# Key/value projection and compressed pages of a decoder step on TensorE: products in fp32 replaced by three products of rounded parts

## What is computed

```
def key_side(h):
    kv = (rms_norm(h, kv_norm) @ w_kv).reshape(B, T, 3, 2, N_KV, HEAD_DIM)      # 1024 -> 3 branches x 512
    return kv[:, :, 0], kv[:, :, 1], kv[:, :, 2]
def seg_proj(seg):                                                            # runs of 16 tokens
    first = jnp.einsum('bsjcgd,cjde->bscge', seg, cmp_w[:, :CMP_STRIDE])
    second = jnp.einsum('bsjcgd,cjde->bscge', seg, cmp_w[:, CMP_STRIDE:])
    return first, second
def compress_blocks(first, second, L):
    blk = first[:, :nc] + second[:, 1:nc + 1] + cbias[:, None, :]
    kc = rms_norm(blk[:, :, 0], k_norm[0])
    return kc, blk[:, :, 1], e_pos
...
past_c = cache_cmp_kv[page_table]         # 8 samples x 32 pages of 128 tokens, 256 KB a page
```

## Time and profile before

| | us |
|---|---|
| median of 3 runs (2642.25 to 2648.58) | 2647.62 |
| the profiled execution, its own time | 2653.37 |
| its span, first to last instruction | 2651.6 |
| TensorE busy | 2437.2 (92%) |
| VectorE busy | 1385.0 (52%) |
| ScalarE busy | 904.4 (34%) |
| GpSimd busy | 774.1 (29%) |

### The profile page before, as it was taken

How to read it: one execution, slowest core, us unless ns; L and a number is a source line. 1 busy time by engine, 2 the same in 40 slices (tenths; PEclk the granted TensorE clock), 3 DMA queues, 4 the chain that set the end, 5 groups by cost and what they waited for, 6 DMA issues and landing times. The chain is left out here.

```text
span 2651.6 us, 62243 instructions
## 1 busy us (share of the span) xinstructions
PE 2437.2 (92%) x25616; PEld 1985.1 (75%) x25616; DVE 1385.0 (52%) x2833; ACT 904.4 (34%) x2023; POOL 774.1 (29%) x460
## 2 busy tenths in 40 slices
PE   5999799986899999989999898997999978999998
PEld 3777699965799999944544385565766677999998
DVE  7216665536577773022233435774777746777600
ACT  2205344315222121110101145765888822222210
POOL 0001000110267665200000023772222204677641
PEclk8999899967899999999999987997999988999999
DMA  2121000012122223151898310005777612222231
GB/s 106 55 64 57 8 4 12 28 39 90 59 72 79 87 74 119 49 221 47 323 326 280 118 58 1 2 1 185 253 251 251 224 64 67 79 87 79 94 99 61
DMA packets 109448, 276.58 MB, mean 104 GB/s; under 512 B 13657, under 2 KB 14554, under 8 KB 107290
## 3 DMA queue, kind: packets, MB, share of 16 engines
q1 hardware_dynamic: 109210, 273.19, 30.5%
HBM read 264.42 MB, written 16.97 MB: 106 GB/s over the span
## 5 line engine op out<-in xcount | busy, mean ns | idle before, releaser
L319 PE MATMUL ps<-parts 128*128 128x288 f32 x6144 | 815.1, 295 | 7.4 <-POOL parts L288 7.4
L319 PEld LDWEIGHTS ps<-parts 128*128 128x128 f32 x6144 | 814.2, 188 | 8.1 <-POOL parts L288 8.1
L288 POOL TENSOR_TENSOR parts<-kept,parts 128x1024 fp32r<-128x1024 f32 (+1 forms) x120 | 320.7, 2673 | 119.5 <-ACT parts L283 112.3
L293 POOL TENSOR_TENSOR parts<-kept 128x1024 fp32r<-128x1024 f32 (+1 forms) x92 | 191.5, 2081 | 378.2 <-DMA kept<-in_wall 188.6
L1660 PE MATMUL ps<-mix,kept 128*128 128x512 f32 (+1 forms) x544 | 228.4, 579 | 0.3 <-DMA mix<-in_cmp_pool 0.3
L1660 PEld LDWEIGHTS ps<-mix,kept 128*128 128x128 f32 x544 | 101.4, 194 | 120.8 <-issue 119.7
L2292 POOL TENSOR_SCALAR mix<-mix 128x128 f32<-128x128 f32 (+3 forms) x128 | 136.7, 1087 | 71.9 <-DVE mix L2266 71.8
L288 POOL TENSOR_TENSOR query_rounded<-mix,query_rounded 128x1024 fp32r<-128x1024 f32 x8 | 16.0, 2000 | 466.8 <-ACT query_rounded L283 466.8
L2769 POOL TENSOR_TENSOR mix<-mix 128x512 f32<-128x512 f32 x64 | 67.0, 1047 | 252.7 <-ACT mix L2793 197.9
L1599 DVE TENSOR_TENSOR kept<-kept,ps 128x576 f32<-128x576 f32 x16 | 12.1, 756 | 245.9 <-PE ps L319 245.9
L702 PE MATMUL ps<-mix 128*128 128x288 f32 x512 | 126.4, 410 | 2.7 <-DVE mix L507 2.4
(11 more groups left out here) (470 smaller groups left out, 4870.0 us busy)
## 6 DMA issues: line engine op xcount, KB each, us to landing
mix<-in_cmp_pool SPq DMA_DIRECT2D x256, 256.0 KB, 4.9
mix<-in_slc_pool SPq DMA_DIRECT2D x192, 256.0 KB, 3.7
kept<-in_wall SPq DMA_DIRECT2D x88, 512.0 KB, 3.5
mix<-in_wall SPq DMA_DIRECT2D x48, 512.0 KB, 3.5
kept<-in_wdown SPq DMA_DIRECT2D x32, 704.0 KB, 4.1
kept<-in_slc_pool SPq DMA_DIRECT2D x64, 256.0 KB, 3.8
out_s_win<-in_state_win SPq DMA_DIRECT2D x1, 8064.0 KB
mix<-in_wkv SPq DMA_DIRECT2D x8, 768.0 KB, 10.3
```

The lines of the kernel that those rows point to most:

```text
L288: return e.tensor_tensor(low.bitcast(F32R), whole, high, ALU.subtract)
L293: e.tensor_tensor(high.bitcast(F32R), whole, c.c("one").to_broadcast([P, whole.shape[1]]), ALU.mult).then_inc(*steps.step())
L319: mm = pe.matmul(out, l[:, f, :].bitcast(F32R), m[:, first + f, a:b].bitcast(F32R), start=first + f == 0 and k == 0, stop=last and f == n ...
```

## The change

The projection runs in three passes over the branches (selected, window, compressed: `passes`), each of 8 pieces of weights of 128x512. ScalarE rounds each piece and each 576-column row of the normed input, GpSimd makes the rest of the weights, VectorE the rest of the input. Each fp32 matmul becomes three of rounded parts. Weights come as 24 DMAs of 256 KB in a ring of four.

The compressor works in units of 11, 11 and 10 pages, 24 units in all, in four buffers (`slot0` to `slot3`). A unit is cut into four quarters. ScalarE rounds a quarter (`high`), VectorE writes the rest of quarters 0 and 2, GpSimd that of quarters 1 and 3, in place over the page (`rest_of`). TensorE runs 12 matmuls of 352 (or 320) columns for a quarter. The rounded copy of a quarter has one buffer for each q, so rounding quarter q of the next unit waits for TensorE to end quarter q of this one. Both halves of the sums are copied from PSUM by VectorE, in 8 copies a unit (`parts`). The copy of 8 MB from `state_win` to `s_win` is issued in the scan, an earlier stage. The other edits (names of the memory parts in `project` and `query`, the page layout in DRAM, SBUF size) leave the instructions of other stages as they are.

```
+            sp.dma_start(d["s_win"][:, 0:WIN - TS, :], d["state_win"][:, TS:, :]).then_inc(*stored.more())
...
-for _n, _k in [("xp", 2 * SEQ * 2), ("raw0", SEG * 512), ("raw1", SEG * 512), ("raw2", SEG * 512)]:
...
+for _k in range(4):
+    CMP.put(f"slot{_k}", 4 * QUARTER)
+for _k in range(4):
+    CMP.put(f"high{_k}", QUARTER)
...
+UNIT_PAGES = (11, 11, 10)
+FIRST_PAGE = (0, 11, 22)
+NU = 3 * NB
...
+    slot = lambda u: (3 + u) % 4
+    count = lambda u: UNIT_PAGES[u % 3]
+    out_of = lambda u: c.ps[{-1: 2, 0: 0, 1: 1}.get(u, 2 + (u + 1) % 2)]
...
+    def load_unit(sp, u):
+
+        if u >= 4:
+            sp.wait_ge(*T.at(seg, f"mm{u - 4}"))
+        first, n = u // 3 * NPG + FIRST_PAGE[u % 3], count(u)
+        for k in range(0, n, 6):
+            pages = c.pages(first + k, min(6, n - k), d["cmp_pool"])
+            for j in range(min(6, n - k)):
+                sp.dma_start(raw[slot(u)][:, k + j].rearrange("p a b -> p (a b)"),
+                             d["cmp_pool"][ds(pages[j], 1)].rearrange("a p n -> (a p) n")).then_inc(
+                                 landed[slot(u)].sem, 16)
...
+    def round_piece(act, z):
+
+        act.wait_ge(piece_got[z % 4].sem, 16 * (z // 4 + 1))
+        if z >= 3:
+            act.wait_ge(*T.at(seg, f"piece{z - 3}"))
+        rounded(act, wraw[z % 4], wpart[z % 3][0]).then_inc(*A.step(f"piece{z}"))
+
+    def round_quarter(act, u, q):
+
+        n = count(u)
+        if q == 0:
+            act.wait_ge(*filled(u))
+        if u >= 1:
+            act.wait_ge(*T.at(seg, f"quarter{u - 1}_{q}"))
+        rounded(act, raw[slot(u)][:, 0:n, q], quarter[q][:, 0:n]).then_inc(*A.step(f"high{u}_{q}"))
+
+    def rest_quarter(e, steps, u, q):
+
+        n = count(u)
+        e.wait_ge(*A.at(seg, f"high{u}_{q}"))
+        rest(e, raw[slot(u)][:, 0:n, q], quarter[q][:, 0:n], rest_of[slot(u)][:, 0:n, q]).then_inc(
+            *steps.step(f"low{u}_{q}"))
...
     def products(pe, u):
 
-        src = xp if u < 0 else raw[u % 3]
-        o = c.ps[2 + u % 2]
-        n = columns(u)[1]
-        if u >= 0:
-            pe.wait_ge(*landed[u % 3].all())
-        if u >= 1:
-            pe.wait_ge(*V.at("cmp", f"part{u - 2}"))
-            pe.wait_ge(*A.at("cmp", f"part{u - 2}"))
+        n, o = count(u), out_of(u)
+        if u >= 4:
+            pe.wait_ge(*V.at(seg, f"part{u - 2}"))
+        if u == 3:
+            pe.wait_ge(*V.at(seg, "part-1"))
+        for q in range(4):
+            k, steps = q // 2, (V, G)[q % 2]
+            pe.wait_ge(*steps.at(seg, f"low{u}_{q}"))
+            for j in range(4):
+                cols = slice(32 * j, 32 * (j + 1))
+                wj = [t[:, (8 * k + 4 * (q % 2) + j) * P:(8 * k + 4 * (q % 2) + j + 1) * P] for t in w_parts]
+                xj = [quarter[q][:, 0:n, cols], rest_of[slot(u)][:, 0:n, q, cols]]
+                for i, (l, r) in enumerate(((0, 0), (0, 1), (1, 0))):
+                    mm = pe.matmul(o[:, 512 * k:512 * k + 32 * n].rearrange("p (n x) -> p n x", x=32),
+                                   wj[l].bitcast(F32R), xj[r].bitcast(F32R),
+                                   start=q % 2 == 0 and j == 0 and i == 0, stop=q % 2 == 1 and j == 3 and i == 2)
+            mm.then_inc(*T.step(f"quarter{u}_{q}"))
+            if q == 3:
+                T.labels[f"mm{u}"] = T.n
...
+    def prompt_products(pe):
+
         for k in range(2):
...
-    def parts(e, steps, copy, u, second):
-
-        lo, n = columns(u)
-        e.wait_ge(*T.at("cmp", f"mm{u}"))
-        dst = f2 if second else f1
-        for par in range(2):
-            for k in range(2):
-                src = c.ps[2 + u % 2][rows[second], 512 * k:512 * k + 4 * n].rearrange(
-                    "p (a o n) -> p a o n", o=2, n=n)[:, :, par]
-                copy(dst[rows[par], 2 * k:2 * k + 2, lo:lo + n], src).then_inc(*steps.step(f"part{u}"))
-
...
+    def parts(v, u):
+
+        v.wait_ge(*T.at(seg, f"mm{u}"))
+        for second, par, k in itertools.product(range(2), repeat=3):
+                dst = (sums if u >= 0 else sums_prompt)[second]
+                if u < 0:
+                    src = out_of(u)[rows[second], 512 * k:512 * k + 4 * n0].rearrange(
+                        "p (a o n) -> p a o n", o=2, n=n0)[:, :, par]
+                    to = dst[rows[par], 2 * k:2 * k + 2, 0:n0]
+                else:
+                    lo, n = 8 * FIRST_PAGE[u % 3], count(u)
+                    src = out_of(u)[rows[second], 512 * k:512 * k + 32 * n].rearrange(
+                        "p (n a o s) -> p o a n s", a=2, o=2, s=8)[:, par]
+                    to = dst[rows[par], 2 * k:2 * k + 2, lo:lo + 8 * n].rearrange("p a (n s) -> p a n s", s=8)
+                v.tensor_copy(to, src).then_inc(*V.step(f"part{u}"))
...
+            for z, (p, f) in enumerate(pieces):
+                if z >= 4:
+                    sp.wait_ge(*G.at(seg, f"piece{z - 4}"))
+                lo = f * 1536 + passes[p] * 512
+                sp.dma_start(wraw[z % 4], d["wkv"][:, lo:lo + 512]).then_inc(piece_got[z % 4].sem, 16)
+                if z == 7:
+                    sp.dma_start(w, d["wcmp"]).then_inc(*got.more())
+                    sp.dma_start(pe_, d["pe"]).then_inc(*got.more())
+                    load_unit(sp, 0)
+                if z == 13:
+                    store_pass(sp, 0)
+                if z == 21:
+                    store_pass(sp, 1)
+            sp.wait_ge(*T.at(seg, "piece23"))
+            load_unit(sp, 1)
+            store_pass(sp, 2)
+            sp.wait_ge(*T.at(seg, "segments"))
+            sp.wait_ge(*stored[2].all())
+            sp.wait_ge(*stored[1].all())
+            sp.wait_ge(*G.at(seg, "values1"))
+            sp.wait_ge(*V.at(seg, "normed1_1"))
+            sp.wait_ge(*T.at(seg, "turned1"))
+            load_unit(sp, 2)
+            sp.wait_ge(*T.at(seg, "bias"))
+            for u in range(3, NU):
+                load_unit(sp, u)
...
+            for z in range(len(pieces)):
+                g.wait_ge(*A.at(seg, f"piece{z}"))
+                rest(g, wraw[z % 4], *wpart[z % 3]).then_inc(*G.step(f"piece{z}"))
+                if z in (10, 18):
+                    p = z // 8 - 1
+                    g.wait_ge(*A.at(seg, f"copied{p}"))
+                    g.wait_ge(*V.at(seg, f"copied{p}"))
+                    g.tensor_copy(vt[:, :, p], kv[p][:, 0:4, 256:]).then_inc(*G.step(f"values{p}"))
+                if z == 20:
+                    g.wait_ge(*A.at(seg, "weights"))
+                    rest(g, w.rearrange("p a b c -> p (a b c)"), *w_parts).then_inc(*G.step("weights"))
...
+                for q in (1, 3):
+                    rest_quarter(g, G, u, q)
...
+                for t, m in tiles:
+                    if p >= 1 and f == 0 and t == 3:
+                        for steps in (V, A):
+                            pe.wait_ge(*steps.at(seg, f"copied{p - 1}"))
+                    xs = [high[:, f, t * P:t * P + m], low_part[f][:, t * P:t * P + m]]
+                    for k, (l, r) in enumerate(((0, 0), (1, 0), (0, 1))):
+                        mm = pe.matmul(own(p, t)[0:m, :], xs[l].bitcast(F32R), wpart[z % 3][r].bitcast(F32R),
+                                       start=f == 0 and k == 0, stop=f == FT - 1 and k == 2)
+                mm.then_inc(*T.step(f"piece{z}"))
...
+            pe.wait_ge(*G.at(seg, "weights"))
+            pe.wait_ge(*V.at(seg, "kept1"))
+            products(pe, 0)
...
+            products(pe, 1)
             pe.wait_ge(*got.all())
-            pe.wait_ge(*V.at("kv", "keys3"))
+            pe.wait_ge(*A.at(seg, "segments"))
...
+            for u in range(2, NU):
                 products(pe, u)
-                if u % 2 == 0:
-                    if u == 0:
-                        pe.wait_ge(*V.at("cmp", "bias"))
-                        turn_keys(pe, 4).then_inc(*T.step("turned4"))
-                    blocks_tensor(pe, u // 2 - 1, NCS if u else NCQ)
-            blocks_tensor(pe, NB - 1, NCS)
+                if u == 2:
...
+            rest_quarter(v, V, 0, 0)
+            rest_quarter(v, V, 0, 2)
+            evict(v, V, v.tensor_copy, 2, 1)
+            rest_quarter(v, V, 1, 0)
+            parts(v, 0)
+            rest_quarter(v, V, 1, 2)
+            rest_quarter(v, V, 2, 0)
+            parts(v, 1)
+            rest_quarter(v, V, 2, 2)
...
+            for u in range(2, NU):
+                if u + 1 < NU:
+                    rest_quarter(v, V, u + 1, 0)
+                if u % 3 == 0:
+                    blocks_vector(v, u // 3 - 1)
+                parts(v, u)
+                if u + 1 < NU:
+                    rest_quarter(v, V, u + 1, 2)
+                if u == 2:
+                    norms_vector(v, -1)
+                if u % 3 == 0:
+                    norms_vector(v, u // 3 - 1)
+            blocks_vector(v, NB - 1)
+            norms_vector(v, NB - 1)
...
+            for q in range(4):
+                round_quarter(act, 0, q)
+            evict(act, A, copy, 2, 0)
```

(41 more changed lines are left out.)

431 lines of the change are left out of this document (226 added, 205 removed).

## The result

| | before | after |
|---|---|---|
| median (lowest to highest), us | 2647.15 (2642.25 to 2648.58) | 2710.67 (2703.03 to 2724.67) |
| profiled execution / its span | 2653.37 / 2651.6 | 2713.92 / 2711.8 |
| the block, VectorE's first square to the end of its last key row | 380.2 | 447.2 |

A forecast was written before the change was run, and what follows sets the result against it. TensorE alone bounds projection and compressor before; afterwards VectorE and GpSimd waiting for each other outweighs the shorter products. The block's +55.2 us on the profiled 2653.4 gives 2708.6, less 5.8 for the median: 2703 us, range 2648 to 2735.

The forecast's parts named there:

- The mechanism: In the compressor, VectorE and GpSimd two-operand SBUF work forms one queue, 31.3 us a sequence, above today's 28.84.
- The walk: One compressor sequence of 32 pages followed instruction by instruction through the engines' in-order queues: 38.3 us for 28.84, range 35.5 to 42.
- Rival A: Compressor rests on VectorE and GpSimd run side by side: 26.4 us a sequence, kernel 2621 us, faster; chance 0.12.
- rival B: Compressor: waiting between VectorE and GpSimd costs only its own 31.3 us a sequence; kernel 2654 to 2665 us; chance 0.14.
- rival C: Compressor: TensorE stays at slow clock between waits of 3 to 7 us; near 48 us a sequence, 2768 us; chance 0.05.
- D: Projection: weights late, TensorE waits at each pass, losing up to its 22 us; given no chance of its own.
- The rounded matmul: TensorE's compressor product of rounded parts: 0.1594 us for 352 columns, with 0.0127 us fixed overhead; 7.65 us a unit.
- GpSimd's 3.24 us: Compressor: GpSimd's time for one rest of 1408 elements, chosen over 2.75 us scaled from a 2.00 us row for 1024.
- the 2691 us: Kernel time if GpSimd's compressor rests took the skill's 2.93 us for 1408 elements, near 1.7 us a sequence shorter.
- The start-up: From projection's end at 1242.3 us through prompt, bias products and first units, with load waits; unit 3 ends at 1306.3.
- The end: End of the changed block: last product at 1564.2 us plus a tail of 12.3, so 1576.5 for 1521.3.
- The moved copy: The 8 MB window copy, moved to the scan: 0, at most a few us if it delays the scan's table.

## Why the prediction was right, point by point

- **The mechanism** held: a rest waits for the other engine's whole rest, VectorE's queue stands behind it, and TensorE waits for VectorE's rest ahead of quarters 2 and for the square ahead of the norm. The walk gave 38.3 us a sequence and the trace has 39.3. Rival A falls by the rows at 1443.85 and by the runs without GpSimd's rests and with all rests on VectorE, rival B since a sequence is 8 us over its 31.3, rival C since the clock is 0.87 to 0.91 in the steady sequences. D falls too: the first product stands at 1156.81 for 1156.3, the matmuls take 0.229 us for 0.226, and the projection ends at 1244.25 for 1242.3.
- **The rounded matmul** is the term that was mis-sized: 0.0127 us over its columns was carried from 288 contiguous columns to 352 in rows of 32, which measured 0.0345. It makes a unit 8.7 us for 7.65, some 3.1 us more work for TensorE in a sequence. The same walk with 0.181 and 0.167 us for a matmul gives 39.1 us, an estimate: the hold covers two thirds of the extra work, and the third that is left is the 1.0 us by which the sequence was short. Rival A's 26.4 us had the same fault; without GpSimd's rests a sequence took 28.2. And it is what makes the idea poor even without a hold: the two kernels that leave half of the rests out take 2636 and 2638 us, fp32 pages 2636.
- **GpSimd's 3.24 us** was right: 3.20 to 3.21 in rows without a hold. The Trainium skill, GPSIMD Engine Reference, section Instruction dispatch, gives about 2.5 cycles an element as the floor; the row of 3.20 us is 2.27 ns, some 2.7 cycles at 1.2 GHz, so here the floor was not reached, and the 2691 us by the Trainium skill's figure were too low. The row of 2.00 us for 1024 is 1.95 ns, 2.3 cycles, which is below that floor; the measurement decides. Of the prediction's two reasons for 3.24 over that row, the size is not the one: in the same trace other rests of 1024 elements on GpSimd (`parts`) take 2.34 us and more. Where the operands lie may be it; no run moved them.
- **The start-up** was 4.7 us short: unit 3 ends at 1311.0 for 1306.3. Unit 1's loads were issued from 1246.06, not from 1242.3, and its eleven issues took 7.04 us for 6.4; three longer units add some 3 us; the prompt's and bias products gave 2 back (7.5 us for 9.5).
- **The end**: 1588.6 for 1576.5. Of these 12.1 us 4.7 are the start-up and some 7 are 6.7 sequences of 1.0 us more, the price of the rounded matmul.
- **The rest of the kernel** was to stay as it was. From the end of the last keys row on, the profile before has 1130 us and the one after 1123, with the same code. The ten profiles of the experiments have between 1120 and 1126 us there, 1124 in the kernel before with only the copy moved; so the 7 us are most likely what one execution differs from another, and the profiled executions lie 60.5 us apart though the blocks lie 67.0 apart.
- **The moved copy** was given 0, with a few us if the scan's table came late. The table was not late (VectorE waited 2.4 us for it with and without), and it cost some 6 us all the same (3 to 10), by another way.
- **The total** came out better than its terms. The block was 12 us longer than forecast and the copy cost some 6 more, which would be 18; by medians the forecast was only 7.7 us low. The changed kernel seems to win back some 10 us outside the block, or its four executions (2703 to 2725 us) fell kindly; no run tells which. So the place in the range was earned by the mechanism and the sequence, and the last 10 us of closeness are luck.

The loss of 63.5 us by medians: the rounded compressor 75 (2710.7 less 2636.0), the copy some 6 to 8, and against them about 18 (2654.3 less 2636.0), the projection's gain less what fp32 pages in units of 11 lose. By the blocks of the profiles it is 81 for the compressor and 15 against it, of 67.

## What to carry to other kernels

When work is split over VectorE and GpSimd, add up the instructions of both that read two operands from SBUF as one queue, as these subtractions had to be, and walk the in-order queue of the engine that others wait for; giving all of it to one engine can beat sharing. Price a cheaper matmul form with the shape and the access pattern that it will have, and compare it with what it replaces before any engine is loaded with its preparation. A large transfer that nobody waits for can still cost time: here it did where TensorE runs over 20 short matmuls in each us, and did not show behind the query.
